# Hyena layers of a fused two-block model: spectral products of a column half split by frequency tile, and the sine layers spread over the input blocks

## The reference, cut to what matters

```python
def hyena_filters(L, w1, b1, wi, bi, w3, freq):
    ...
    h = jnp.sin(fr * (z @ w1.astype(f32) + b1.astype(f32)))
    for j in range(HY_INNER):
        h = jnp.sin(fr * (h @ wi[j].astype(f32) + bi[j].astype(f32)))
    h = h @ w3.astype(f32)
    ...
    return k / jnp.sum(jnp.abs(k), axis=0, keepdims=True)

def long_conv(u, kf):
    L = u.shape[1]
    U = jnp.fft.rfft(u, n=2 * L, axis=1)
    return jnp.fft.irfft(U * kf[None], n=2 * L, axis=1)[:, :L]

def hyena_mixer(...):
    p = xn @ w_in + b_in
    p = conv_b + sum(pp[:, j:j + L] * conv_w[j] for j in range(HY_SHORT))
    x1, x2, v = jnp.split(p, 3, axis=-1)
    kf = jnp.fft.rfft(hyena_filters(...), axis=0)
    for o, gate in enumerate((x1, x2)):
        z = gate.astype(f32) * (long_conv(z, kf[:, o]) + fbias[o].astype(f32) * z)
    return z.astype(xn.dtype) @ w_out + b_out
```

## Time and profile before

| | |
|---|---|
| median of 3 runs | 4742.24 us (4738.83 to 4742.59) |
| the profiled execution | 4747.01 us, span 4745.2 us |
| PE busy | 4281.9 us, 90% of the span |
| DVE busy | 2014.6 us, 42% |
| ACT busy | 1221.1 us, 26% |
| POOL busy | 1442.0 us, 30% |
| mean granted clock of PE | 0.93 |
| Hyena layers in the trace | from 20 to about 510 us and from 2032 to about 2517 us |

### The profile page before, as it was taken

The page is one execution under the profiler, slowest core; times in us unless marked ns, Lnnn a source line. Parts: engine busy times, 40 slices in busy tenths (PEclk is TensorE's granted clock), DMA queues, the critical chain, the costliest instruction groups (busy, mean ns, idle before and its releaser), DMA issues.

```text
span 4745.2 us, 47608 instructions
## 1 busy us (share of the span) xinstructions
PE 4281.9 (90%) x19046; PEld 3151.0 (66%) x19046; DVE 2014.6 (42%) x2985; ACT 1221.1 (26%) x1699; POOL 1442.0 (30%) x834
## 2 busy tenths in 40 slices
PE   7987999899999599989979997888986999998998
PEld 5655788556788388866557886556665665685777
DVE  6466233264413631365563232456663146403322
ACT  3322212134222122233222121322320224422221
POOL 3311344100443144433113442256563000231343
PEclk9998999999999799999989997889996889999999
DMA  6100222211232123211002322021201121121232
GB/s 170 71 27 9 98 102 84 98 45 36 89 111 85 45 102 116 86 61 71 27 17 97 105 81 75 29 56 29 56 15 49 55 81 63 65 95 62 80 96 73
DMA packets 96909, 333.71 MB, mean 70 GB/s; under 512 B 44337, under 2 KB 47537, under 8 KB 67889
## 3 DMA queue, kind: packets, MB, share of 16 engines
q1 hardware_dynamic: 87968, 311.85, 19.2%
q10 hardware_dynamic: 8720, 18.82, 1.6%
HBM read 317.53 MB, written 13.11 MB: 70 GB/s over the span
## 4 chain that ended last, share of the span: by engine, by line
PE 80%; DVE 13%; ACT 2%; POOL 2%; issue 2%; DMA 1%; SPq 0%; DVEq 0%; ACTq 0%; POOLq 0%
PE bank L873 16%; PE bank L874 16%; PE bank L875 16%; PE bank L1215 5%; PE bank L853 4%; PE bank L1029 4%; PE bank L862 2%; PE bank L1003 1%; PE bank L1527 1%; PE bank L981 1%; DVE xn L2211 1%; PE bank L1526 1%; PE bank L1455 1%; PE bank L1548 1%; PE bank L1324 1%
## 5 line engine op out<-in xcount | busy, mean ns | idle before, releaser
L768 POOL TENSOR_TENSOR w_lo<-ring,w_hi 128x2048 fp32r<-128x2048 f32 (+2 forms) x200 | 774.0, 3870 | 1621.4 <-ACT w_hi L1682 1621.4
L873 PE MATMUL bank<-x_hi,w_hi 128*128 128x512 f32 x1664 | 659.8, 397 | 51.2 <-DVE x_lo L2194 47.1
L874 PE MATMUL bank<-x_lo,w_hi 128*128 128x512 f32 x1664 | 652.9, 392 | 0.0
L875 PE MATMUL bank<-x_hi,w_lo 128*128 128x512 f32 x1664 | 652.8, 392 | 0.0
L1682 ACT ACTIVATE w_hi<-ring 128x2048 fp32r<-128x2048 f32 (+2 forms) x200 | 321.9, 1610 | 947.9 <-PE bank L875 947.0
L873 PE MATMUL bank<-h_hi,w_hi 128*128 128x512 f32 x960 | 382.4, 398 | 35.7 <-DVE h_lo L2200 35.7
L873 PEld LDWEIGHTS bank<-x_hi,w_hi 128*128 128x128 f32 x1664 | 315.1, 189 | 137.3 <-issue 43.6
L874 PE MATMUL bank<-h_lo,w_hi 128*128 128x512 f32 x960 | 380.9, 397 | 0.0
L875 PE MATMUL bank<-h_hi,w_lo 128*128 128x512 f32 x960 | 380.4, 396 | 0.0
L875 PEld LDWEIGHTS bank<-x_hi,w_lo 128*128 128x128 f32 x1664 | 315.6, 190 | 66.7
L874 PEld LDWEIGHTS bank<-x_lo,w_hi 128*128 128x128 f32 x1664 | 316.0, 190 | 63.3
(11 more groups left out here) (418 smaller groups left out, 7277.3 us busy)
## 6 DMA issues: line engine op xcount, KB each, us to landing
ring<-stream SPq DMA_DIRECT2D x212, 1024.0 KB, 4.8
ring<-stream SPq DMA_DIRECT2D x64, 704.0 KB, 4.0
ring<-stream SPq DMA_DIRECT2D x36, 512.0 KB, 3.6
xn<-first_mods SPq DMA_DIRECT2D x8, 1024.0 KB, 5.9
ring<-stream SPq DMA_DIRECT2D x4, 1088.0 KB, 5.0
bias_rows<-work ACTq DMA_DIRECT2D x1, 4096.0 KB, 46.8
work<-bias_rows ACTq DMA_DIRECT2D x1, 3072.0 KB, 11.5
tab<-tabs ACTq DMA_DIRECT2D x1, 2624.0 KB, 16.7
```

What stands on the lines that cost most here:

```text
L768: nc.gpsimd.tensor_tensor(w_lo[:, j % 2, 0:cols], ring[:, k % RING, 0:cols], w_hi[:, j % 2, 0:cols], ALU.subtract).then_inc(wlo_set, 1)
L873: mm(b[:], hi[:, at + k, :], rhs_hi, start=(k == 0), stop=False)
L874: mm(b[:], hi[:, at + k, :], rhs_lo[:, k, :], start=False, stop=False)
L875: ins = mm(b[:], lo[:, at + k, :], rhs_hi, start=False, stop=(k == kt - 1))
```

## The change

It does two things, in both Hyena layers.

1. `multiply` takes a second argument, the frequency tiles it covers. DVE's order in a stage becomes: drain tile 0 of the signal, multiply the first column half for tile 0, drain tile 1, multiply the first column half for tile 1 (this sets `prod_set`), multiply the second column half for both tiles. PE's and ACT's lists are as before in this part.
2. The sine layers stand before blocks 0, 3 and 6 on PE, ACT and DVE, and `stack_sines` stands before DVE's `shorts(15)`, where it was `shorts(6)`.

```diff
+SINE_BLOCKS = (0, 3, 6)
...
                 for j in range(11):
-                    if j < 3:
-                        sine_layer(j)
+                    if j in SINE_BLOCKS:
+                        sine_layer(SINE_BLOCKS.index(j))
                     block(in_hi[j], x_hi_h, xn_r, (xn_set, n["xn"] - DT) if j == 0 else None)
...
-                    if j in (0, 2, 4):
-                        sine_layer(j // 2)
-                    if j == 6:
+                    if j % 2 == 0 and j // 2 in SINE_BLOCKS:
+                        sine_layer(SINE_BLOCKS.index(j // 2))
+                    if j == 2 * SINE_BLOCKS[-1] + 3:
                         stack_sines()
...
-                    spectra(U)
-                    multiply(0)
-                    multiply(1)
+                    spectra(U, (0,))
+                    multiply(0, slice(0, 1))
+                    spectra(U, (1,))
+                    multiply(0, slice(1, 2))
+                    multiply(1, slice(0, 2))
...
-            def multiply(half):
+            def multiply(half, fs):
...
-                signal(stt(s_, s_, 2.0, d_, ALU.mult, ALU.subtract), prod_set)
+                last = stt(s_, s_, 2.0, d_, ALU.mult, ALU.subtract)
+                if fs.stop == 2:
+                    signal(last, prod_set)
+                else:
+                    step(last)
```

More of the change, by code:

```diff
@@ L2348, in spectra @@
                 dve.wait_ge(aux_drained[aux.place(t)], aux.turn(t) + 1)
-            def multiply(half):
+            def multiply(half, fs):
                 cs = slice(256 * half, 256 * (half + 1))
-                a, b = [ctmp[:, j].rearrange("p a (b c) -> p a b c", b=2) for j in range(2)]
+                a, b = [ctmp[:, j].rearrange("p a (b c) -> p a b c", b=2)[:, fs] for j in range(2)]
                 Uv, Kv = [v.rearrange("p (f k r) c -> p f k r c", f=2, k=2) for v in (U, K)]
-                ur, us, kr, ks = [v[:, :, k, :, cs] for v in (Uv, Kv) for k in range(2)]
+                ur, us, kr, ks = [v[:, fs, k, :, cs] for v in (Uv, Kv) for k in range(2)]
                 tt_(a, us, ks, ALU.mult)
@@ L2361, in multiply @@
                 step(tt_(us, us, b, ALU.add))
-                both = U.rearrange("p (g r) c -> p r g c", r=2)
+                both = U[:, 4 * fs.start:4 * fs.stop, :].rearrange("p (g r) c -> p r g c", r=2)
                 s_, d_ = both[:, 0, :, cs], both[:, 1, :, cs]
                 step(tt_(d_, s_, d_, ALU.subtract))
-                signal(stt(s_, s_, 2.0, d_, ALU.mult, ALU.subtract), prod_set)
+                last = stt(s_, s_, 2.0, d_, ALU.mult, ALU.subtract)
[3 more added lines that the diff above has]
+                    step(last)
             def attention(s):
```

## The result

| | before | changed |
|---|---|---|
| median, 6 runs each | 4742.32 us (4738.49 to 4743.48) | 4707.9 us (4703.36 to 4730.63) |
| ratio | | 0.9937, 95% interval 0.9918 to 0.9956 |
| profiled execution | 4747.01 us, span 4745.2 | 4707.1 us, span 4705.3 |
| PE busy, mean clock | 4281.9 us, 0.93 | 4257.2 us, 0.937 |

The forecast was 4714, in a range of 4704 to 4724. The gains of the three medians, 34.4, 20.4 and 24.9 us, have a mean of 26.6; 28.2 was forecast. All three medians lie in the range of the forecast, and each interval leaves 1 out; the first measurement alone makes the change look better than the three together do.

What follows compares the result with a forecast made beforehand. PE, 80% of the chain, was taken to bound the kernel where it waits or runs at 1.2 GHz. Products 9.8, stage 3 6.6 and sine layers 11.8 sum to 28.2 us off the median: 4714 us, range 4704 to 4724.

Steps and rivals of the forecast that it cites:

- The half product and the earlier products: Stages 0 to 2: a half product takes 5.48 us, and both products of a stage come 2.9 us earlier.
- The clock behind the 2.5 us wait: Stages 0 to 2: a fall costs 1.69 us, six in eight; six stages gain 9.8 us, bounds 7.3 and 17.4.
- Rival 1: The clock holds in most of the 2.5 us waits: gain 32 to 37 us, time 4708; chance 0.15.
- Stage 3: Last stage of each layer: POOL's hold on DVE takes 3.8 to 4.3 us; gain 3.3, two stages 6.6.
- One reading behind this step: L2234 reads a bank and `xn` beside POOL's feed-forward weight work, and its 88 take 690 to 692 ns, not held.
- The sine layers: Input blocks: PE's waits for a sine go; gain 5.7 and 6.1 us, sum 11.8, bounds 10.1 and 12.3.
- rival 2: Input blocks: sine gain partly lost to late loads or ACT's copies, all clocks fall; gain 18 to 23 us, chance 0.14.
- Rival 4: Products: the half product is no cheaper than the whole, up to 32 us slower, 4774; chance 0.02.
- rival 3: Stage's end: the products' earlier end buys nothing, something else ends last; gain near 12 us, time 4730; chance 0.05.
- rival 5: Whole kernel: no effect, as list order does not set the times; within 9.5 us; chance 0.03.

Runs made afterwards that it cites:

- shifted: Changed kernel with two unread matmuls of 0.86 us ahead of the first filter's spectra in both Hyena layers; 4720.35 us, ratio 0.9952 to the kernel before.
- products_only: Changed kernel with the sine layers back before blocks 0, 1 and 2, the products split and interleaved; 4730.18 us, ratio 0.9973 to the kernel before.
- sine_late: Changed kernel with the sine layers before blocks 1, 4 and 7 instead of 0, 3 and 6; 4710.14 us, ratio 0.993 to the kernel before.
- after_again: The changed kernel measured a second time, no edit; 4722.67 us, ratio 0.9963 to the kernel before.
- sine_only: Changed kernel with the products put back as before, sine layers still before blocks 0, 3 and 6; 4726.27 us, ratio 0.9967 to the kernel before.
- split_late: Kernel before with the first column half's products split by frequency tile, both halves behind all the signal's drains; 4752.93 us, ratio 1.0022.
- warm_both: As warm_wait, with one more unread matmul ahead of each of the magnitudes' sums; 4712.85 us, ratio 0.9939 to the kernel before.
- warm_wait: Changed kernel with two unread matmuls before PE's second wait in stages 0 to 2; 4707.54 us, ratio 0.9924 to the kernel before.

## Why the prediction was right, point by point

**The half product and the earlier products: right.** A half product takes 5.44 us (taken 5.48). PE's waits are 1.35 and 2.53 us (1.4 and about 2.5) in all six stages of every trace of the changed kernel, and L1030 waits for no bank.

**The clock behind the 2.5 us wait: somewhat under-priced.** The step took six in eight; it was six of six, in all three traces. By that the term is 7.3 and not 9.8. Rival 1 is out for this kernel; in shifted one of the six such waits left the clock up, in products_only and sine_late none. The six stages shared one fate in all three launches; what varied lay outside them. What the sum left out is that a fall can also come behind the sums, or not, for a whole layer: before, each layer had one there in each of stages 0 to 2 (L1003 at 8.8 in place of 7.1, behind stage 2 L1029 at 16.3 in place of 14.0), the changed kernel none in the first layer and a longer one in the second. A stage so gained 3.1 us in the first and lost 0.35 in the second (starts of L1029 at 218.25 and 282.82, L1030 at 209.55 and 271.06; 2225.49 and 2290.02, 2198.40 and 2263.30). The mean, 1.4 a stage, is near the forecast's 1.6 by a cancellation the forecast didn't contain.

**Stage 3: right in its mechanism.** POOL's instruction begins as DVE drains banks, and holds only the product behind them:

```profile
2401.86 0.69 DVE L2349 TENSOR_TENSOR work<-work,bank 128x512 f32<-128x512 f32 x1
2402.47 0.68 DVE L2350 TENSOR_TENSOR work<-work,bank 128x512 f32<-128x512 f32 x1
2403.25 4.36 DVE L2359 TENSOR_TENSOR work<-work,xn 128x512 f32<-128x512 f32 x1
...
2402.55 4.51 POOL L793 TENSOR_TENSOR ring_r<-ring,hyena_hi 128x2048 fp32r<-128x2048 f32 x1 [73.44 <-ACT hyena_hi L1695]
```

4.36 - 0.69 = 3.7 us of hold where it had been 4.3, just outside the 3.8 to 4.3 of the forecast, and PE waits 11.89 instead of 15.52: 3.6 gained, 3.3 taken. POOL's instruction itself took 4.51 us and not 5.00.

One reading behind this step was wrong: the earlier trace rows shows nothing of what runs beside POOL, since none of the 88 cases of L2234 overlaps an instruction of POOL's. Nor does the changed kernel test it: its last drain, L2350, had begun 0.08 us before POOL's instruction, as L2356 had begun before it in the old order and took its usual 1.23. Other rows of the kernel before bear the step out. L2627, which reads a bank and `work`, began beside an instruction of POOL's in 64 of 80 cases and took 0.35 us, as everywhere else. Four of 16 of L2224, which reads a bank and `x`, began beside one as well, at their usual 0.75:

```profile
471.35 4.61 POOL L792 TENSOR_TENSOR ring_r<-ring,hyena_hi 128x2048 fp32r<-128x2048 f32 x1 [12.88 <-ACT hyena_hi L1694]
474.97 0.75 DVE L2224 SCALAR_TENSOR_TENSOR x<-bank,vec,x 128x512 f32<-128x512 f32 x1 [4.84 <-PE bank L875]
```

**The sine layers: right.** Forecast 5.7 and 6.1; the traces of the changed kernel show 5.3 to 5.8 and 5.7 against the first trace before, 4.9 to 5.4 and 5.7 against the second. The new waits at blocks 1 and 2 are 2.16, 0.88 and 1.75 us; in two of its three traces the clock fell behind the first of them and the second vanished, the two outcomes that the step had named. No wait for a late load, so rival 2's mechanism did not occur. Rival 4 is refuted by 0.69 us an instruction, rival 3 by the first layer, whose stages are 3.1 us shorter, rival 5 by the moved waits and the three intervals.

**The total.** In the three traces of the changed kernel the input projections and stages together are 27 us shorter than in the first trace before, 23 than in the second; 28.2 was forecast, and the three medians average 26.6. The first median's extra 6 us were not repeated. The forecast took nothing for the rest of the kernel and the stretches between; in the first trace they gave 12.3 of 39.9 us, which no step foresaw. So the closeness of 26.6 to 28.2 is in part luck: the waits were forecast well, but the clock added or took several us in places that the sum left out. The trace of after_again is of its fastest execution (4712.19 us, the others 4718 to 4730), so what the slower ones lost is not seen here.

## What to carry to other kernels

Where a producer waits for its last operand, put the part of the next step that needs only the first operands into that wait, and price the split by two rows: here 1.2 us of extra instructions bought 4.2 us of overlap a stage. Before counting a shortened wait of PE in full, look at what each remaining one does to the clock: here a bridged wait handed its fall on to the next weak stretch, and small changes ahead of four stages, of 1 to 2 us, moved them by 8 to 12. A result of a few tenths of a per cent needs the same stretches compared over several traces; here one median of six runs was 15 us from another of the same kernel.

## What the runs showed of the hardware that was not expected

The place of a clock fall repeats. In the changed kernel the stages of one layer share one form, and it recurs in three traces (268.1 and 278.7 us, to 0.1), while the stretch behind them varies by 7 us between the same traces. It is not so in every kernel: in shifted, sine_only, split_late and warm_both the stages of a layer differ (in sine_only's second layer 64.6 and 62.8 us). Small changes ahead of the stages switched the form by 8 to 12 us a layer, in either direction. Behind a wait of 2.53 us the clock fell in 35 of 36 cases (the changed kernel's three traces, products_only, sine_late and shifted), behind one of 1.35 us in none of these.

The magnitudes' sums show no gap on PE (3.63 us, 32 matmuls of 128x1), and the clock can fall behind them all the same: it did in stages 0 to 2 of the kernel before and of warm_wait, not in those of the changed kernel's first layer. One dense matmul of 0.86 us ahead did not prevent it.
